# A two-layer decoder trunk on one core, with TensorE's filler products left out

## The reference, cut to what matters

```python
for layer in range(DEPTH):
    z = rms_norm(h, norm_mix[layer]) @ w_in[layer]
    ...                                    # y: state space, convolution, attention
    h = h + y @ w_out[layer]
    h = h + cross_attention(rms_norm(h, norm_cross[layer]), rms_norm(mem, norm_mem[layer]), ...)
    hn = rms_norm(h, norm_ffn[layer])
    if layer % 2 == 0:
        h = h + swiglu(hn, ffn_w_up[layer // 2], ffn_w_down[layer // 2])
    else:
        h = h + moe_swiglu(hn.reshape(bsz * seq, d), moe_router[layer // 2], moe_w_up[layer // 2],
                           moe_w_down[layer // 2]).reshape(bsz, seq, d)

def moe_swiglu(x2, w_router, w_up, w_down):
    logits = (x2 @ w_router).astype(jnp.float32)
    top_val, top_idx = lax.top_k(logits, TOP_K)
    gate = jax.nn.softmax(top_val, axis=-1)
    ...                                    # each expert: up, SwiGLU, down on its own tokens
```

## Time and profile before

| | |
|---|---|
| median of three runs | 1279.03 us (1276.59 to 1281.38) |
| profiled execution, span | 1276.7 us |
| TensorE matmul busy | 1234.3 us, 97% of the span |
| VectorE busy | 700.9 us, 55% |
| ScalarE busy | 428.9 us, 34% |
| GpSimd busy | 99.6 us, 8% |
| moved by DMA | 360.97 MB, mean 283 GB/s |
| mean granted clock of TensorE | 0.994 of full speed |

### The profile page before, as it was taken

One profiled execution on the slowest core, in us unless ns is written; L12 is line 12 of the kernel. 1 busy time (PEld: TensorE's weight loads), 2 busy tenths in 40 slices (PEclk: granted clock), 3 DMA queues, 4 the chain that ended last, 5 costly groups with the idle time before them and its releaser, 6 DMA issues.

```text
span 1276.7 us, 49013 instructions
## 1 busy us (share of the span) xinstructions
PE 1234.3 (97%) x21610; PEld 1050.2 (82%) x21610; DVE 700.9 (55%) x1629; ACT 428.9 (34%) x884; POOL 99.6 (8%) x157
## 2 busy tenths in 40 slices
PE   7999998999999999999899999999999999999897
PEld 5765566877887776556699999999999999999896
DVE  7876435657866376642455555555545455554445
ACT  4526413001002131642334333333333333333232
POOL 1360110000000045011000000000000000000010
PEclk9999899999999999999999999999999999999999
DMA  9620025243442553514699999999999999999994
GB/s 372 237 95 39 1 105 208 100 192 114 190 178 87 201 197 120 220 50 182 220 382 425 425 426 425 427 426 425 425 428 426 425 425 425 427 426 425 427 422 164
DMA packets 36571, 360.97 MB, mean 283 GB/s; under 512 B 4163, under 2 KB 5827, under 8 KB 11548
## 3 DMA queue, kind: packets, MB, share of 16 engines
q1 hardware_dynamic: 33776, 354.86, 67.5%
q10 hardware_dynamic: 2156, 3.19, 0.7%
q0 software_dynamic: 576, 2.10, 0.4%
HBM read 356.77 MB, written 3.36 MB: 282 GB/s over the span
## 4 chain that ended last, share of the span: by engine, by line
PE 79%; DMA 7%; DVE 3%; issue 1%; ACT 1%; SPq 1%; POOL 1%; DVEq 0%; ACTq 0%
PE bank L2497 25%; PE bank L1869 18%; PE bank L2514 13%; DMA ring<-moe_w_dram 7%; PE bank L2440 6%; PE bank L2222 4%; PE bank L2484 2%; PE bank L1877 2%; PE bank L2210 1%; PE bank L2151 1%; PE bank L2239 1%; SPq L544 1%; PE bank L2533 1%; PE bank L1900 1%; PE bank L1914 1%
## 5 line engine op out<-in xcount | busy, mean ns | idle before, releaser
L2497 PE MATMUL bank<-R,ring 128*64 128x80 f32 x11264 | 427.3, 233 | 9.6 <-DVE ring L1763 7.8
L2497 PEld LDWEIGHTS bank<-R,ring 128*64 128x64 f32 x11264 | 405.9, 137 | 15.9 <-DVE ring L1763 13.4
L1869 PE MATMUL bank<-ring 128*128 128x128 f32 (+2 forms) x1776 | 287.7, 321 | 1.6 <-ACT ring L664 0.9
L1869 PEld LDWEIGHTS bank<-ring 128*128 128x128 f32 x1776 | 242.8, 191 | 49.3 <-issue 36.6
L2514 PE MATMUL bank<-zz,ring 128*64 128x80 f32 x5632 | 226.8, 234 | 0.0
L975 ACT ACTIVATE ring<-ring 128x1024 f32<-128x1024 f32 x160 | 169.1, 1057 | 137.2 <-PE bank L2514 137.2
L2514 PEld LDWEIGHTS bank<-zz,ring 128*64 128x64 f32 x5632 | 210.0, 138 | 0.0
L1814 DVE SCALAR_TENSOR_TENSOR zz<-zz,bank 128x80 f32<-128x80 f32 x176 | 42.0, 238 | 174.4 <-PE bank L2497 173.6
L1763 DVE COPY ring<-ring 128x1024 f32<-128x1024 f32 x160 | 110.4, 690 | 18.1 <-DMA ring<-moe_w_dram 17.9
L980 ACT ACTIVATE sqx<-bank 128x80 f32<-128x80 f32 x176 | 41.7, 237 | 221.4 <-PE bank L2497 218.8
L1767 DVE COPY ring<-ring 128x1024 f32<-128x1024 f32 x160 | 109.8, 686 | 0.2 <-DVE R L1753 0.2
(11 more groups left out here) (338 smaller groups left out, 1139.8 us busy)
## 6 DMA issues: line engine op xcount, KB each, us to landing
ring<-moe_w_dram SPq DMA_DIRECT2D x158, 1536.0 KB, 21.6
ring<-ffn_w_dram SPq DMA_DIRECT2D x11, 3072.0 KB, 10.1
ring<-w_in_dram SPq DMA_DIRECT2D x6, 2048.0 KB, 8.0
extra<-moe_w_dram SPq DMA_DIRECT2D x8, 1536.0 KB, 23.2
ring<-w_out_dram SPq DMA_DIRECT2D x4, 2048.0 KB, 7.8
ring<-w_small_dram SPq DMA_DIRECT2D x2, 3072.0 KB, 11.1
ring<-w_x_dram SPq DMA_DIRECT2D x2, 3072.0 KB, 10.9
ring<-w_in_dram SPq DMA_DIRECT2D x2, 2144.0 KB, 15.5
```

Source lines behind the costliest of these rows:

```text
L1869: i = pe.matmul(out_ap, a, b, start=(k == 0), stop=(k == n - 1))
L2497: e = pe.matmul(pb[out_bank][c0:c0 + 64, 0:CAP], half[:, P * k + c0:P * k + c0 + 64], xg[:, k], start=(k == 0), stop=(k == KT - 1), tile_p ...
```

## The change

All fillers but `warm_first` go, and so do their entries in the table of banks. Nothing else is edited; what stood behind a filler now stands behind what stood ahead of it.

```diff
@@ plan_banks
-        if l:
-            a("warm_mix", 3, 0)
         for g in range(5):
             a(f"mix_T{g}_", MIX_BANKS[g])
...
-        a("warm_ffn", 3, 0)
         for g in range(5):
             a(f"ffn_T{g}_", FFN_BANKS[g])
...
-            add("warm_router", 0, 0); add("router", 2)
-            add("warm_count", 0, 0); add("count", 3); add("warm_pick", 1, 0)
+            add("router", 2)
+            add("count", 3)
@@ TensorE's program
-                if l:
-                    keep_warm(f"warm_mix{l}", 7)
                 norm_tiles("mix_T", l, NORM[f"mix{l}"])
...
-                keep_warm(f"warm_ffn{l}", 3)
                 norm_tiles("ffn_T", l, NORM[f"ffn{l}"], (0, 1))
...
                 if i:
-                    keep_warm("warm_router", 2)
                     norm_tiles("ffn_T", 1, NORM["ffn1"], (2, 3, 4))
                 wait_tile("ffn_T", 1, (2, 3, 4) if i else (0, 1))
                 e = halved(ps(nm)[:, 8 * i:8 * i + 8], [(xT[:, k, P * i:P * i + P], rt[:, k]) for k in range(KT)])
             done(nm, e)
-            keep_warm("warm_count", 3)
             nm = "count"
...
-            keep_warm("warm_pick", 2)
             HALVES = (0, 64)
```

## The result

The changed kernel takes 1284.42 us in the median of nine runs (1282.18 to 1286.88). The kernel before, run beside it, takes 1280.12 (1276.59 to 1282.17, nine runs). The ratio is 1.0031, with a 95% interval of 1.0018 to 1.0044: about 4.0 us slower by the ratio (4.3 by the two medians), inside the 0.5% that was set as the bound of "same", but clear of no change. It lies within the stated range of 1276 to 1287, and 0.4 us beyond the 1278.5 to 1284 that the prediction gave its forecast by itself.

The account below looks back on a forecast made before the run. TensorE's chain (79%) bounds the kernel, the expert loop its weights. -0.45 - 0.3 + 1.1 - 1.45 + 4.0 = +2.9 us on the profiled 1276.7; about two thirds put on the median of 1279.03 gave 1281.0, range 1276 to 1287.

Parts of the forecast that it names:

- its forecast: Clock falls at the router, in some executions at layer 1's mixer: 1281.0 us, by itself 1278.5 to 1284; chance 0.50.
- each feed-forward start: Layer 0's feed-forward and layer 1's router: without three fillers, the first transposes start earlier, 0.45 us won at each.
- the 1.0 us between the tiles: Layer 1's router: without the two fillers between the halves, tile 1's transposes follow the first half directly, winning 1.0 us.
- The sum of 2.2: Whole kernel, clock unchanged: 0.45 at layer 0, 0.3 at the mixer and 1.45 at the router won.
- the router's cost, taken at 4.0 us: Layer 1's router to gather: a likely clock fall soon after the first transposes costs 4.0 us, bounds 0 and 8.1.
- four parts: Router at lower clock: second transposes 0.8, second router half 1.1, count products 0.9, gather 1.9; together 4.7 us.
- more than 10 us at the lower clock around the router: Sign in the profile after that would show the forecast wrong and point to the fourth rival.
- the fourth rival: Clock stays low long at layer 1's mixer and from router through first expert tile: +9.3 us, 1288.3; chance 0.15.
- The mixer's even chance: Layer 1's mixer start: a 2.1 us idle gap makes the clock fall half the time, 0.5 x 2.2 = 1.1 us.
- The 2.9: Whole kernel: gains and clock costs sum to +2.9 us on the profiled execution's 1276.7, so 1279.6.
- The second: Rival for the whole kernel: the clock doesn't fall, fillers only stood in the way; -2.2 us, 1276.8; chance 0.20.
- The third: Rival at the expert loop: weights loaded ahead hide what happens at the router; only +0.35 remains, 1279.4; chance 0.15.

Follow-up runs that it names:

- the front alone: Against the kernel before, layer 0's three feed-forward and layer 1's mixer's seven fillers left out, the router's ten kept: 1280.85 us, ratio 1.0004.
- the kernel with fitted fillers: Kernel before with fillers refitted to waits: one per feed-forward start, five at the mixer, the router's two on the path gone, others added in its waits: 1278.45 us, ratio 0.9985.
- the thin fillers: Kernel before with all fillers except the three in front 8 columns wide in place of 256, same number and place: 1285.82 us, ratio 1.0049.
- the fillers in the router's waits only: Changed kernel plus five fillers ahead of the count and two ahead of the gather; timed against the kernel before: 1283.86 us, ratio 1.0025.

## Why the prediction was right, and where it was off

**The mechanism** was the one forecast: with the clock unchanged the change wins, the falls cost more, and the router decides. Leaving out the router's fillers alone costs 2.6 us, the front's alone nothing that could be measured, and five products inside waits alone cost 3.1 us. The mean granted clock of whole runs says the same beyond the profiles: 0.984 to 0.989 in the nine runs of the changed kernel, 0.992 to 0.997 in the 52 of before beside the experiments.

**What it wins.** 0.45 us for each feed-forward start became 0.35 and 0.37; the 1.0 us between the tiles shows as 0.97 in the kernel with fitted fillers. At the mixer that kernel won 0.22 for a forecast of 0.3, though it removed only two of seven fillers. The sum of 2.2 was right to about 0.3 us. One reading under it was loose: by their rows the fillers ahead of the count end at 629.46 and those ahead of the gather at 632.48, and the gather of before starts without a wait. So the last two may hold it up by some 0.1 us (an estimate: the count's 1.25 and the 0.80 us of DVE's pick would let it start 2.05 us behind the count, not 2.15).

**What was mis-sized: the router's cost, taken at 4.0 us.** By the ledger it was 6.5 in the profiled execution: the first products +0.65 (the step to the second transposes was -0.29, where the kernel without the router's fillers, whose clock was still up there, won 0.94), the second transposes +0.94, the second products +0.77, the count +0.92, the gather +2.10, and the first expert tile 4.19 in place of 2.43, of which +1.11 reached the second tile. I had priced four parts to about 0.3 us (0.8, 1.1, 0.9, 1.9) but cut their sum because "part of the gather will run at full clock again", and had the first products and the first expert tile only in the upper bound of 8.1. The step that failed is the fall's length: "soon after the first transposes, and lasting until the gather gives dense work again". In the profile the clock fell as the first products began (1.75 us in place of 1.10) and came back at 642 us, behind the first expert tile: the gather and nearly all of the tile ran at 0.50. By the prediction's own sign, "more than 10 us at the lower clock around the router", that is the fourth rival's router and not the forecast's. The reason given against that rival, that dense work ended every fall in the trace of before, was misread for the fall at 137 us: the eight transposes at 142.59 us still ran at the low clock (1.88), the two 512-column matmuls behind them took the same 1.02 us in before and after, so the fall was over before the dense output products began at 145.96. The kernel without the router's fillers, where it came back within the gather, shows that the cut fits some executions; its 2.6 us by the ratio is what was forecast for the router, 4.0 - 1.45 = 2.55.

**The mixer's even chance** was too low: all four profiles of kernels without its seven fillers of 256 columns fell there (the changed one, the front alone, the thin fillers, and the fillers in the router's waits only), and none of the other six, which have seven or five. The price was small: +0.58 in the changed kernel and +0.97 with the front alone, with the 0.2 to 0.3 won there 0.8 to 1.3 us, against 2.2 taken for a fall. So the term 0.5 x 2.2 = 1.1 came out by luck, a chance too low times a price too high.

**On the median** I put two thirds of the sum, with the reason that some runs of before fall in the router already. Neither profile of before shows that. The reason rested on 2.3 us between the median and the profiled span, and most of that is no fall: in every run on record that has both figures, the time lies 1.8 to 2.0 us above the span. The 2.9 as worked out would have been nearer to the 4.0 measured. The predicted 1281.0 was low by 3.4 us, of which 1.1 lies in the median of before, 1280.12 by nine runs and not 1279.03. It is the width of the range, made to take in most of the way to the fourth rival, that held the result.

**The rivals.** The second (no fall) is refuted by 0.50 from 622 to 642 us. The third (the loop hides it) is refuted by the ledger: +3.94 at the second tile, +3.95 at the last group of matmuls, and 425 GB/s throughout. The fourth described the profiled execution's router better than the forecast did, but its mixer cost a fifth to a third of the 3.1 us it reckoned. The Trainium skill's advice to leave no idle gaps between bursts of products ("TensorE: Matmul & The Clock Gate", section "Why this matters for your kernels") is borne out in its direction. In the length of gap that it lets pass it isn't: every wait of TensorE in the changed kernel's router is shorter than that, the longest 2.29 us, and the clock fell.

## What to carry to other kernels

A filler is worth its place when it fits into a wait, and costs its time where it doesn't: read the wait's length from the timeline, fill that, and leave the path free. Don't judge a stretch by its longest gap alone (the thin fillers left no wait over 1.32 us, and the clock fell), and look for what runs behind it at the low clock; here a gather and the first tile of a loop paid most, and a loop bound by transfers never gave it back. Fill early: the fillers that came after the fall ran slow themselves, 4.64 us in place of 2.43. And look for other gaps of the kind: the two in the attention, which the kernel had left open, were worth about as much as all the fitting elsewhere, 2.1 against 1.9 us by the ratios.

## What the runs showed of the hardware

In this router products of 8 columns in the gaps did not hold the clock, products of 256 columns at the same places did: 0.50 for 20 us against 1.00. The same gap of 1.80 us, behind the same work, fell in some executions and not in others of the same kernel. And falls lasted differently: 3.4 us at the mixer (0.57 over 4 us), with products of 256 columns behind the transposes, and 20 us in the router, through a gather of 64 products (4.53 us) and an expert tile of 64 more (4.19 us) that left TensorE 0.74 us of wait between them.
